# First block of a two-block network: attention passes begin after four of eight input projections, with the rest set between the passes

## The chip, the cores and the metric

One core of a Trainium2 chip runs the whole kernel in one launch. The metric is the time of one execution on the device in microseconds (us); the span is the time from the first to the last instruction of a profiled execution.

## The reference, cut to what matters

Two blocks work on 256 tokens of width 1024. The first (`first_block`) is computed once; its token mixing is what the change is about:

```python
mod = jax.nn.silu(c) @ w_ada[l] + b_ada[l]            # 6 rows of 1024: shifts, scales, gates
h  = rmsnorm(x,  g_mix[l]) * (1.0 + sc1) + sh1
hc = rmsnorm(xc, g_mix[l]) * (1.0 + csc1) + csh1      # 256 context tokens, used as keys and values
p = h @ w_in                                          # 1024 -> 2048
qa = axial_rope(heads(OFF_AQ, OFF_AK, A_HEADS, A_DH), rows, cols)   # 8 query heads of 64
ka = axial_rope(heads(OFF_AK, OFF_AV, A_KV, A_DH), rows, cols)      # 2 key heads of 64
ya = window_sink_attn(qa, ka, va, ka_c, va_c, sink)   # 128-token blocks, window 128, and 256 context keys
yb = chunk_gmlp(p[..., OFF_BU:OFF_BV], p[..., OFF_BV:OFF_CQ], ws, bs, gtok)
yc = diff_out(diff_attn(q1, q2, k1, k2, vall, lam), gsub, lam_init)  # 4 heads, two softmaxes each
y = jnp.concatenate([ya, yb, yc], axis=-1) @ w_out
x = x + gt1 * y
x = x + gt2 * hier_moe(h2, ...)                       # 16 experts, 2 of a group per token
```

The second block has two layers, each a SwiGLU FFN (1024 to 2 x 2816), a token mixing with three attentions (its q, k, v projection is 12 units of 256 columns) and another FFN. Each layer's nine modulation rows come from `cond @ ada_w[l] + ada_b[l]`. Everything is fp32.

## The kernel before, in words

Weights are streamed from memory by one DMA queue, issued by SyncE in an order that is written out. A *unit* is 128 x 2048 fp32 (1 MB). ScalarE rounds it (`conv_hi`, L270), VectorE makes the rest (`conv_lo`, L276), and TensorE multiplies in three products (`mm3`, L343 to L345). Three units fit (`RING`), so the load of unit c waits for `conv_lo` of unit c-3.

The modulation rows of both blocks (12 + 36 *halves* of 512 outputs) are made from a stream of its own. A half is 2 MB in two parts, and each part has one buffer, `ada[:, 0]` and `ada[:, 1]`, which it must leave before the next half can be loaded into it. For halves 0 to 3, TensorE multiplies directly (L1109). For all later ones VectorE does eight steps of 128x512 (`half_step`, L304 and L310), then TensorE sums over the partitions with four one-column products (`half_sum`, L324; each fp32 product stands as two rows in the trace), and VectorE adds the bias (`half_out`, L338). They are placed beside other work: halves 4 to 9 beside the early projections, 10 to 19 beside the attention passes, the rest beside the FFNs of the second block.

The input projection of the first block is eight units (`IN_UNITS`): 0 gives keys and values A, 1 and 2 the queries A, 3 keys C, 4 values C, 5 queries C, 6 and 7 the inputs of the gated MLP. Units 0, 3 and 4 are also multiplied with the context, so there are eleven projections of two tiles. Units 0 to 5 (`EARLY_UNITS`) come first. GpSimd rotates queries and keys (`rope`), TensorE turns them (`turn_pair`, L1137), and then 32 attention passes run, one per head and query block: 16 of kind A (the window) and 16 of kind C (the two softmaxes). Iteration i of the loop issues on TensorE the scores of pass i (L1158, in kind A behind a mask product L1157 of 512 columns), the turning of the probabilities of pass i-1 (L1165), and the product with the values of pass i-2 (L1174). VectorE takes the maximum (L1493), ScalarE the exponential (L1280) and the copy (L1287). In kind A query and key stand on 64 rows, since a head is 64 wide. Between the passes stand the projections of units 6 and 7 (`B_TURNS`), the turning of queries and keys C (from iteration `C_TURN0`), the gated MLP, the half sums (`ATT_SUMS`), and on VectorE some two or three half steps each. After the last pass of a group of eight, `finish` scales the output; behind the last one and behind the last half sum TensorE turns the result (`turn`, L409) and multiplies with `w_out`. TensorE executes its instructions in order; so do the others.

In the second block the loops over FFN groups and over q, k, v units are hardware loops (`Fori`).

## Time and profile before

| | us |
|---|---|
| median of 3 runs (lowest to highest) | 2260.92 (2258.34 to 2265.45) |
| the profiled execution | 2261.06 |
| its span | 2259.3 |
| busy: TensorE, VectorE, ScalarE, GpSimd | 2008.0, 1388.1, 998.5, 91.7 |
| mean granted TensorE clock | 0.924 of 2.4 GHz |

The span holds the whole program; the first block's mixing takes about its first 335 us. Shares of busy time are averages over stages with different limits, so each stage has to be read by itself. A TensorE that is busy at half clock counts as busy. The clock has two levels in the trace, written 1.00 and 0.50.

### The profile page before, as it was taken

To read this page: it belongs to the slowest core of one execution; us is meant where nothing else is said; L and a number is where in the kernel's file an instruction comes from. 1 tells how busy PE (TensorE), PEld (TensorE's weight loads), DVE (VectorE), ACT (ScalarE), POOL (GpSimd) and SP (SyncE) were. 2 spreads that over 40 slices of the span, in tenths; PEclk is the share of its full clock that TensorE was granted. 3 is DMA by queue.
4 is the path that set the end of the run, shared out by engine and by line. 5 is a ranking of instruction groups with operands and counts; after the bars stand their busy time and mean duration, and the time that the engine had idled before them with its cause. 6 is when DMAs were issued, how large, how long until landed. Compare 5 with 4: busy or idle time off the path is not lost.

```text
span 2259.3 us, 31283 instructions
## 1 busy us (share of the span) xinstructions
PE 2008.0 (89%) x12630; PEld 1769.3 (78%) x12630; DVE 1388.1 (61%) x1440; ACT 998.5 (44%) x1149; POOL 91.7 (4%) x103
## 2 busy tenths in 40 slices
PE   6878977999999699988797799989998979968997
PEld 1855667888888699978776689978997967857997
DVE  0875755899998677754433677766765343355445
ACT  2423324777777433344345343343334433444333
POOL 0230010000000100010000000000001000000000
PEclk9876786999999899989898899999999989989999
DMA  7563452899998287634312457755763532223553
GB/s 271 199 231 111 164 207 76 324 370 358 348 352 337 114 322 297 254 124 174 106 63 75 149 220 282 283 218 208 299 238 131 176 109 108 75 77 133 191 183 150
DMA packets 63845, 457.93 MB, mean 203 GB/s; under 512 B 7040, under 2 KB 7296, under 8 KB 8832
## 3 DMA queue, kind: packets, MB, share of 16 engines
q1 hardware_dynamic: 63744, 456.51, 53.4%
q8 instruction: 72, 1.18, 0.2%
q14 instruction: 29, 0.24, 0.0%
HBM read 455.43 MB, written 1.05 MB: 202 GB/s over the span
## 4 chain that ended last, share of the span: by engine, by line
issue 40%; PE 39%; DVE 10%; ACT 5%; DMA 3%; POOL 1%; DVEq 1%; POOLq 1%; SPq 0%; ACTq 0%
PE PS L343 10%; PE PS L344 10%; PE PS L345 10%; DVE wlo L276 3%; ACT whi L270 3%; DVE acc L310 2%; DMA ada<-in_ada 2%; PE PS L1158 1%; PE PS L324 1%; DMA raw<-in_stream 1%; PE PS L1701 1%; PE PS L1109 1%; PE PS L1174 1%; POOLq L396 1%; POOL st L397 1%
## 5 line engine op out<-in xcount | busy, mean ns | idle before, releaser
L276 DVE TENSOR_TENSOR wlo<-raw,whi 128x2048 fp32r<-128x2048 f32 x285 | 653.7, 2295 | 514.3 <-ACT whi L270 514.3
L270 ACT ACTIVATE whi<-raw 128x2048 fp32r<-128x2048 f32 x285 | 545.0, 1913 | 496.9 <-PE PS L345 461.1
L343 PE MATMUL PS<-whi,hhi 128*128 128x256 f32 (+1 forms) x1360 | 450.6, 331 | 18.1 <-DVE hlo L466 8.6
L344 PE MATMUL PS<-wlo,hhi 128*128 128x256 f32 (+1 forms) x1360 | 441.4, 325 | 0.0
L345 PE MATMUL PS<-whi,hlo 128*128 128x256 f32 (+1 forms) x1360 | 441.3, 324 | 0.0
L343 PE MATMUL PS<-hhi,whi 128*128 128x256 f32 x1408 | 402.2, 286 | 10.3 <-DVE mod L338 7.7
L344 PE MATMUL PS<-hlo,whi 128*128 128x256 f32 x1408 | 400.2, 284 | 0.0
L345 PE MATMUL PS<-hhi,wlo 128*128 128x256 f32 x1408 | 400.1, 284 | 0.0
L343 PEld LDWEIGHTS PS<-whi,hhi 128*128 128x128 f32 x1360 | 266.5, 196 | 41.1 <-DVE hlo L466 10.1
L343 PEld LDWEIGHTS PS<-hhi,whi 128*128 128x128 f32 x1408 | 272.0, 193 | 14.2 <-DVE wlo L276 8.9
L345 PEld LDWEIGHTS PS<-whi,hlo 128*128 128x128 f32 x1360 | 265.6, 195 | 19.2
L344 PEld LDWEIGHTS PS<-wlo,hhi 128*128 128x128 f32 x1360 | 266.5, 196 | 17.7
L344 PEld LDWEIGHTS PS<-hlo,whi 128*128 128x128 f32 x1408 | 272.1, 193 | 1.4
L345 PEld LDWEIGHTS PS<-hhi,wlo 128*128 128x128 f32 x1408 | 272.0, 193 | 0.0
L343 PE MATMUL PS<-whi,zr 128*128 128x512 f32 (+2 forms) x624 | 233.0, 376 | 21.0 <-DVE zr L1936 11.1
L310 DVE SCALAR_TENSOR_TENSOR acc<-ada,cs,acc 128x512 f32<-128x512 f32 x308 | 238.6, 775 | 10.8 <-DMA ada<-in_ada 1.4
L345 PE MATMUL PS<-whi,zr 128*128 128x512 f32 (+2 forms) x624 | 228.4, 369 | 0.0
L344 PE MATMUL PS<-wlo,zr 128*128 128x512 f32 (+2 forms) x624 | 228.2, 369 | 0.0
L343 PEld LDWEIGHTS PS<-whi,zr 128*128 128x128 f32 (+1 forms) x624 | 114.8, 184 | 41.7 <-DVE zr L1936 11.2
L345 PEld LDWEIGHTS PS<-whi,zr 128*128 128x128 f32 (+1 forms) x624 | 114.7, 184 | 20.8
L344 PEld LDWEIGHTS PS<-wlo,zr 128*128 128x128 f32 (+1 forms) x624 | 114.9, 184 | 18.8
L276 DVE TENSOR_TENSOR wlo<-ada,whi 128x2048 fp32r<-128x2048 f32 x48 | 109.9, 2292 | 12.7 <-ACT whi L270 12.5
(349 smaller groups left out, 1895.5 us busy)
## 6 DMA issues: line engine op xcount, KB each, us to landing
raw<-in_stream SPq DMA_DIRECT2D x285, 1024.0 KB, 4.8
ada<-in_ada SPq DMA_DIRECT2D x96, 1024.0 KB, 4.8
ada<-in_stream SPq DMA_DIRECT2D x48, 1024.0 KB, 4.9
xs<-in_x SPq DMA_DIRECT2D x1, 1024.0 KB, 7.7
Z<-in_ctx SPq DMA_DIRECT2D x1, 1024.0 KB, 9.8
masks<-in_masks SPq DMA_DIRECT2D x2, 512.0 KB, 6.8
Z<-in_gfinal SPq DMA_DIRECT2D x2, 512.0 KB, 7.4
y_out<-Z SPq DMA_DIRECT2D x2, 512.0 KB, 2.6
```

What stands on the lines that cost most here:

```text
L270: nc.scalar.activation(whi[:, s], src, ACT.Copy).then_inc(hi_ready, 1)
L276: nc.vector.tensor_tensor(wlo[:, s], src, whi[:, s].bitcast(F32), ALU.subtract).then_inc(lo_ready, 1)
L310: ins = nc.vector.scalar_tensor_tensor(a, w, c, a, ALU.mult, ALU.add)
L324: ins = nc.tensor.matmul(PS[:, bank, c:c + 1], acc[:, v % 2, c * P:(c + 1) * P], ones[:, 0:1], start=True, stop=True)
L343: nc.tensor.matmul(out_, ah, bh, start=start, stop=False, skip_group_check=check)
L344: nc.tensor.matmul(out_, ah, bl, start=False, stop=False, skip_group_check=check)
L345: return nc.tensor.matmul(out_, al, bh, start=False, stop=stop, skip_group_check=check)
L396: pool.drain()
L397: nc.gpsimd.tensor_tensor(st[:, 4 + t:5 + t], st[:, 2 + t:3 + t], k1[:, K1["half"]][:, 0:1], ALU.pow).then_inc(*N.rstd.up)
L1109: ins = nc.tensor.matmul(PS[0:2, 6 + v % 2, :], cs[:, n:16:8], ada[:, i, 512 * k:512 * k + 512], start=n == 0, stop=n == 7)
L1158: nc.tensor.matmul(PS[:, i % 2], q, k, start=i >= 16, stop=True).then_inc(*s_mm.up)
L1174: ins = nc.tensor.matmul(PS[:, 4 + (p // 8) % 2, 64 * (p % 8):64 * (p % 8) + 64], pt[:, p % 2, c * P:(c + 1) * P], v[c], start=c == 0, sto ...
```

## The change

1. Only units 0 to 3 are projected before the first pass. Units 4 to 7 (ten tiles) stand between the passes, in iterations 0 to 10 (`FILL_TURNS`), all through PSUM bank 7. SyncE's order of loads follows.
2. VectorE rotates the queries and keys A; GpSimd keeps those of C, in two pieces.
3. The keys of each kind-A head are held in a tile of their own, filled up to 128 rows with zeros, so that all scores have 128 rows. The mask product comes behind the scores and has 256 columns.
4. Halves 4 to 10 are done as before (three steps per iteration, up to half 10). Halves 11 to 17 (`SPLIT_HALVES`) are shared: VectorE does the first part (two steps per iteration, from iteration 16), TensorE the second with sixteen one-column products (`half_direct`, eight per iteration, from iteration 17), and four that add VectorE's part (`half_rest`). Halves 18 and 19 move: the first FFN of layer 0 takes 18 to 27, and 28 and 29 stand in layer 0's q, k, v projection.
5. The turning of C's queries and keys, the gelu and the gated MLP stand five or six iterations later.
6. The hardware loops of the second block are written out.

The diff, cut to its core:

```diff
-EARLY_HALVES = 20
-FFN_HALVES = {(0, 0): (20, 10), (0, 1): (30, 10), (1, 0): (40, 8), (1, 1): (48, 0)}
+EARLY_HALVES = 18
+SPLIT_HALVES = range(11, EARLY_HALVES)
+FFN_HALVES = {(0, 0): (18, 10), (0, 1): (30, 10), (1, 0): (40, 8), (1, 1): (48, 0)}
+QKV_HALVES = (28, 29)
...
+        ak = [z(6656, 512).rearrange("p (s n) -> p s n", s=2), xn[:, :, 768:1024]]
...
+        def half_free(v, i):
+            if v < PE_HALVES:
+                return ada_used_pe, 2 * v + i + 1
+            if v in SPLIT_HALVES and i:
+                return ada_used_pe, pe_used(v) + 1
+            return ada_used, dve_used(v) + i + 1
...
+        def half_direct(pe, v, bank, m):
+            cond = 0 if v < B1_HALVES else 16
+            if m == 0:
+                pe.wait_ge(ada_landed[1], 16 * (v + 1))
+                pe.wait_ge(*ada_out.at(v - PE_HALVES - 1))
+            c, k = m // 4, m % 4
+            ins = nc.tensor.matmul(PS[:, bank, c:c + 1], ada[:, 1, 512 * k + P * c:512 * k + P * c + P],
+                                   cs[:, cond + 4 + k:cond + 5 + k], start=m == 0, stop=False, skip_group_check=True)
+            if m == 15:
+                ins.then_inc(ada_used_pe, 1)
+        def half_rest(pe, v, bank):
+            pe.wait_ge(*half_free(v, 0))
+            for c in range(4):
+                ins = nc.tensor.matmul(PS[:, bank, c:c + 1], acc[:, v % 2, c * P:(c + 1) * P], ones[:, 0:1],
+                                       start=False, stop=True, skip_group_check=True)
+            ins.then_inc(*ada_sum.up)
...
-        EARLY_UNITS = 6
+        EARLY_UNITS = 4
...
-        B_TURNS = {0: (6, 0), 1: (6, 1), 3: (7, 0), 4: (7, 1)}
-        C_TURN0, GELU_TURN, GM_TURN = 6, 6, 12
+        ATT_V0, ATT_FULL = PE_HALVES + 1, SPLIT_HALVES[0]
+        ATT_STEPS = 3
+        SPLIT_PE, SPLIT_DVE = 17, 15
+        FILL_TURNS = {0: (4, "c", 0), 1: (4, "c", 1), 2: (4, "x", 0), 3: (4, "x", 1), 5: (5, "x", 0), 6: (5, "x", 1),
+                      7: (6, "x", 0), 8: (6, "x", 1), 9: (7, "x", 0), 10: (7, "x", 1)}
+        C_TURN0, GELU_TURN, GM_TURN = 11, 12, 18
...
-                    if i < 16:
-                        nc.tensor.matmul(PS[:, i % 2], idb[:, :], masks[:, i // 8], start=True, stop=False)
-                    nc.tensor.matmul(PS[:, i % 2], q, k, start=i >= 16, stop=True).then_inc(*s_mm.up)
+                    ins = nc.tensor.matmul(PS[:, i % 2], q, k, start=True, stop=i >= 16, skip_group_check=i < 16)
+                    if i < 16:
+                        ins = nc.tensor.matmul(PS[:, i % 2, 256:512], idb[:, :], masks[:, i // 8, 256:512], start=False, stop=True,
+                                               skip_group_check=True)
+                    ins.then_inc(*s_mm.up)
...
+                h, r = divmod(i - SPLIT_PE, 2)
+                if 0 <= h < len(SPLIT_HALVES):
+                    for m in range(8 * r, 8 * r + 8):
+                        half_direct(pe, SPLIT_HALVES[h], 6, m)
+                    if r:
+                        half_rest(pe, SPLIT_HALVES[h], 6)
...
+            for v, units in ((4, (3,)), (5, (4,)), (6, (5, 6, 7)), (7, (8, 9)), (8, (10,)), (9, (11,))):
+                for u in units:
+                    load(sp, u)
                 load_half(sp, v)
```

The three places where the order matters most follow.

TensorE at the start of the passes before. L343 to L345 are the last products of unit 5, L324 two half sums, L1137 the turning of queries and keys A, L1157 the mask, L1158 the first scores:

```order
L343 MATMUL PS<-whi,hhi 128x256
L344 MATMUL PS<-wlo,hhi 128x256
L345 MATMUL PS<-whi,hlo 128x256
L324 MATMUL PS<-k,acc 128x1 x8
L1137 MATMUL PS<-k,Z 128x128 x12
L1157 MATMUL PS<-masks,idb 128x512
L1158 MATMUL PS<-Z 128x512
```

The same place now. L372 to L374 are the last products of unit 3, and those with zr belong to unit 4 and the context:

```order
L373 MATMUL PS<-wlo,hhi 128x256
L374 MATMUL PS<-whi,hlo 128x256
L1146 MATMUL PS<-k,Z 128x128 x12
L338 MATMUL PS<-k,acc 128x1 x4
L1168 MATMUL PS<-Z 128x512
L1170 MATMUL PS<-masks,idb 128x256
L372 MATMUL PS<-whi,zr 128x256
```

The first scores now stand ahead of units 4 and 5, and the mask product behind them.

TensorE in the kind-C passes before (scores, turning, values, and every third or fourth pass a half sum):

```order
L1158 MATMUL PS<-Z 128x512
L1165 MATMUL PS<-k,Z 128x128 x4
L1174 MATMUL PS<-Z 128x64 x4
L324 MATMUL PS<-k,acc 128x1 x4
L1158 MATMUL PS<-Z 128x512
L1165 MATMUL PS<-k,Z 128x128 x4
L1174 MATMUL PS<-Z 128x64 x4
```

The same passes now, two of them, which make up one shared half:

```order
L1168 MATMUL PS<-Z 128x512
L1179 MATMUL PS<-k,Z 128x128 x4
L1188 MATMUL PS<-Z 128x64 x4
L349 MATMUL PS<-cs,ada 128x1 x8
L1168 MATMUL PS<-Z 128x512
L1179 MATMUL PS<-k,Z 128x128 x4
L1188 MATMUL PS<-Z 128x64 x4
L349 MATMUL PS<-cs,ada 128x1 x8
L358 MATMUL PS<-k,acc 128x1 x4
```

Twenty one-column products stand in two passes, where four stood in three or four.

VectorE beside the early projections before (L276 is `conv_lo`, L304 and L310 are the steps of a half):

```order
L276 TENSOR_TENSOR wlo<-raw,whi 128x2048
L304 TENSOR_SCALAR acc<-ada,cs 128x512
L310 SCALAR_TENSOR_TENSOR acc<-ada,cs,acc 128x512 x7
L276 TENSOR_TENSOR wlo<-raw,whi 128x2048
L304 TENSOR_SCALAR acc<-ada,cs 128x512
L310 SCALAR_TENSOR_TENSOR acc<-ada,cs,acc 128x512 x7
```

Now, from the `conv_lo` of unit 4 on; L748 to L754 are a rotation:

```order
L278 TENSOR_TENSOR wlo<-raw,whi 128x2048
L325 SCALAR_TENSOR_TENSOR acc<-ada,cs,acc 128x512 x4
L748 TENSOR_TENSOR Z<-Z,k 128x128
L749 TENSOR_TENSOR Z<-Z,k 128x128
```

One half instead of six is done there, and three rotations stand between the conversions.

## Rows read from the trace of the kernel before

**Rows 1.** Stages: us, busy by engine (instructions), granted clock, DMA share, GB/s.
```profile
143.90:183.60 39.70, 34.42 (x202) 25.07 (x202) 19.99 (x35) 12.48 (x24) 0.00 (x0) 0.93 0.34 122
183.60:240.80 57.20, 53.03 (x174) 35.61 (x175) 29.40 (x63) 19.45 (x44) 1.66 (x1) 0.50 0.30 106
240.80:291.40 50.60, 46.38 (x277) 35.32 (x277) 40.52 (x71) 20.96 (x50) 1.02 (x1) 0.89 0.52 187
...
1000.00:1035.00 35.00, 35.00 (x294) 35.00 (x293) 14.20 (x7) 14.38 (x12) 0.00 (x0) 1.00 0.50 184
```

**Rows 2.** Timeline of ScalarE, early projections: start, us, instruction, idle before and releaser.
```profile
91.11 0.60 ACT L1252 ACTIVATE Z<-PS 128x512 f32<-128x512 f32 x1 [3.36 <-PE PS L345]
97.59 1.92 ACT L270 ACTIVATE whi<-raw 128x2048 fp32r<-128x2048 f32 x1 [5.88 <-DMA raw<-in_stream]
```

**Rows 3.** Timeline of VectorE, early projections and passes.
```profile
115.73 5.54 DVE L310 SCALAR_TENSOR_TENSOR acc<-ada,cs,acc 128x512 f32<-128x512 f32 x7
...
178.13 2.29 DVE L276 TENSOR_TENSOR wlo<-raw,whi 128x2048 fp32r<-128x2048 f32 x1 [3.62 <-ACT whi L270]
...
218.03 0.69 DVE L1493 TENSOR_REDUCE sm<-PS 128x1 f32<-128x512 f32 x1 [3.33 <-PE PS L1158]
```

**Rows 4.** Timeline of TensorE, start of the passes.
```profile
136.78 1.84 PE L324 MATMUL PS<-k,acc 128*128 128x1 f32 x8 [9.75 <-DVE mod L338]
...
143.87 0.58 PE L1157 MATMUL PS<-masks,idb 128*128 128x512 bf16 x1 [2.59 <-issue]
```

**Rows 5.** Timeline of TensorE, kind-A passes at the low clock.
```profile
224.51 2.07 PE L1158 MATMUL PS<-Z 64*128 64x512 f32 x2
...
229.02 0.63 PE L1157 MATMUL PS<-masks,idb 128*128 128x512 bf16 x1
...
234.09 0.63 PE L1157 MATMUL PS<-masks,idb 128*128 128x512 bf16 x1
```

**Rows 6.** Timeline of TensorE, kind-C passes at the high clock.
```profile
245.02 1.08 PE L1158 MATMUL PS<-Z 128*128 128x512 f32 x2
245.94 0.60 PE L1165 MATMUL PS<-k,Z 128*128 128x128 f32 x4
...
247.21 1.08 PE L1158 MATMUL PS<-Z 128*128 128x512 f32 x2
...
251.64 1.00 PE L324 MATMUL PS<-k,acc 128*128 128x1 f32 x8
252.50 1.10 PE L1158 MATMUL PS<-Z 128*128 128x512 f32 x2
```

**Rows 7.** The chain of waits, a load of one part of a half.
```profile
253.19 4.75 DMA ada<-in_ada
```

**Rows 8.** Timeline of TensorE, last scores and the end of the passes.
```profile
286.50 1.08 PE L1158 MATMUL PS<-Z 128*128 128x512 f32 x2
...
302.58 1.86 PE L324 MATMUL PS<-k,acc 128*128 128x1 f32 x8 [10.09 <-DVE acc L310]
304.31 3.65 PE L409 MATMUL PS<-k,xn 128*128 128x128 f32 x16
```

**Rows 9.** Timeline of TensorE, around two falls of the clock.
```profile
277.53 1.12 PE L1165 MATMUL PS<-k,Z 128*128 128x128 f32 x4 [3.56 <-ACT Z L1280]
...
389.33 2.29 PE L877 MATMUL PS<-sm,Z 128*128 128x4 f32 x20
```

**Rows 10.** Stretches around a rise and a fall, and narrow products; columns as in rows 1.
```profile
283.00:284.00 1.00, 1.00 (x12) 1.00 (x10) 0.96 (x2) 1.00 (x3) 0.00 (x0) 1.00 0.01 0
...
355.00:361.00 6.00, 6.00 (x29) 6.00 (x29) 0.00 (x0) 0.00 (x0) 0.00 (x0) 0.50 0.35 145
388.00:389.00 1.00, 1.00 (x6) 0.84 (x5) 0.40 (x1) 1.00 (x1) 0.00 (x0) 1.00 1.00 426
392.00:393.00 1.00, 1.00 (x7) 1.00 (x6) 1.00 (x2) 0.00 (x0) 0.00 (x0) 0.50 0.39 148
```

More of the change, by code:

```diff
@@ L632, in hidden_act @@
             act_hi(act, 0, None, E0, h0)
[L633 removed]
+            for g in range(1, FFN_GROUPS):
+                steps, sums = g < nh, g <= nh
+                c = at_gate(c0, g)
+                conv_hi(act, c + RING, E0)
+                act_silu(act, g, c0, E0, h0)
+                conv_hi(act, c + 1 + RING, E0)
+                act_hi(act, g, c - 1, E0, h0)
+                conv_hi(act, c + 2 + RING, E0)
         def hidden_dve(dve, c0, E0, h0, halves):
             v0, nh = halves
[L638 to L650 removed]
             conv_lo(dve, c0 + RING, E0)
@@ L659, in hidden_dve @@
                 half_steps(dve, v0, 1)
-            hidden_loop(dve, body, nh)
+            for g in range(1, FFN_GROUPS):
+                steps, sums = g < nh, g <= nh
+                c = at_gate(c0, g)
+                conv_lo(dve, c + RING, E0)
+                if steps:
+                    half_steps(dve, v0 + g, 0)
+                dve_h(dve, g, h0)
+                conv_lo(dve, c + 1 + RING, E0)
+                dve_lo(dve, g, h0)
+                if sums:
+                    half_out(dve, v0 + g - 1, 2 * (1 - g % 2))
+                if steps:
+                    half_steps(dve, v0 + g, 1)
+                conv_lo(dve, c + 2 + RING, E0)
         N1, N3 = Norm("n1", 3), Norm("n3", 2, stats_only=True)
@@ L745, in a_scores @@
             if p < 16:
-                r = slice(64 * (j % 2), 64 * (j % 2) + 64)
                 kv = j % 2
@@ L1258, in turned_out @@
                 act.wait_ge(*t1_mm.at(i))
+                if i < 2:
+                    for kv in range(2):
+                        r = slice(64 * kv, 64 * kv + 64)
+                        ins = nc.scalar.activation(ak[kv][r, i], PS[r, bank, 0:256], ACT.Copy)
+                    ins.then_inc(*t1_out.up)
+                    return
                 if i not in (8, 11):
@@ L1415, in normalise_v @@
                 dve.drain()
-                sq = xn[:, :, 0:256]
+                sq = row[:, 0:512].rearrange("p (t n) -> p t n", t=2)
+                dve.wait_ge(*rope_c.at(1))
                 for t in range(NT):
@@ L1617, in pe_layer @@
                 project(unit(pe, QK0 + j, E0), hhi, hlo, j, lo_at=None if j else lo_at(1, l)).then_inc(unit_used, 1)
-            with pe.Fori(0, 3) as i:
-                for j in range(3):
-                    pe.wait_ge(B["q_out"].sem, l * 12 + i * 3 + (j + 1))
-                    project(unit(pe, QK0 + 3 + j, E0 + i), hhi, hlo, j).then_inc(unit_used, 1)
+            for j in range(3, 12):
+                pe.wait_ge(*B["q_out"].at(j - 3, l))
+                project(unit(pe, QK0 + j, E0), hhi, hlo, j % 3).then_inc(unit_used, 1)
+                if l == 0 and j in (6, 10):
+                    half_sum(pe, QKV_HALVES[j // 10], 3)
             def gate_unit(f, bank, tile=None):
@@ L1886, in dve_layer @@
             conv_lo(dve, FF0 + FFN_UNITS - 1 + RING, E0)
-            with dve.Fori(0, 4) as i:
-                for j in range(3):
-                    conv_lo(dve, QK0 + j + RING, E0 + i)
+            for j in range(12):
+                conv_lo(dve, QK0 + j + RING, E0)
+                if l == 0 and 1 <= j <= 8:
+                    v, n = QKV_HALVES[(j - 1) // 4], 2 * ((j - 1) % 4)
+                    if n == 6 and v > QKV_HALVES[0]:
+                        half_out(dve, v - 1, 3)
+                    half_step(dve, v, n)
+                    half_step(dve, v, n + 1)
+            if l == 0:
+                half_out(dve, QKV_HALVES[1], 3)
             dve.wait_ge(*B["q_out"].at(11, l))
@@ L2121, in _ @@
                 hidden_sp(sp, FF0, E0, FFN_HALVES[l, 0])
-                with sp.Fori(0, MIX_UNITS // RING) as e:
-                    for j in range(RING):
-                        load(sp, QK0 + RING + j, E0 + e)
+                for j in range(MIX_UNITS):
+                    if l == 0 and j in (1, 5):
+                        load_half(sp, QKV_HALVES[j // 5])
+                    load(sp, QK0 + RING + j, E0)
                 hidden_sp(sp, FF1, E0, FFN_HALVES[l, 1])
```

336 lines of the change are left out of this document (159 added, 177 removed).

## The prediction

> **What bounds the kernel now.** I read the stages first (the stretches with busy time and clock), then the timelines of single engines in the first 310 us, and the chain of waits for what a DMA costs there. Nearly all of the change lies in that part.
>
> In the passes TensorE is busy 34.42 of 39.70 us, then 53.03 of 57.20, then 46.38 of 50.60, and its clock is 0.93, 0.50 and 0.89 [rows 1]. So the middle stretch is TensorE at half clock: one kind-A pass takes 5.07 us (229.02 to 234.09), its scores on 64 rows 2.07 [rows 5]. A kind-C pass at the high clock takes 2.19 us, 245.02 to 247.21, and there VectorE works 40.52 of 50.60 us [rows 1, 6]. Ahead of the passes TensorE waits for VectorE: 9.75 us before a half sum, first mask at 143.87 [rows 4]. Behind them it waits 10.09 us for the last half, and turns the result at 304.31 [rows 8]. These two waits and the low clock can be won back. The reader should keep four marks: first pass 143.87, scores of pass 17 at 245.02, of pass 31 at 286.50, turning at 304.31.
>
> **The change part by part.** I build the same four marks for the changed kernel.
>
> *The start.* The fourth of the six projections that remain is copied out at 91.11 [rows 2]; one takes about 5.8 us (rows 2: idle 3.36 and what ScalarE does between), so unit 3 with its context ends at 91 + 2 x 5.8 = 102.6. Then the last rotation on VectorE decides. It stands behind the `conv_lo` of unit 5, whose load is queued on SyncE behind the second part of half 5, and that waits for four steps of half 4, which stand behind a rotation of about 3 us (twelve instructions, my estimate from the 0.69 us of 512 columns in rows 3: 0.25 each). Before, this unit landed at 97.59 [rows 2]; five later, say 103. With the two conversions (1.92 and 2.29, rows 2 and 3) and 3.2 us of rotation it is 110; turning, a half sum at the low clock (1.73: 302.58 to 304.31, rows 8) and the copies add 2.5. First pass at 112.7; bounds 108 (load in time) and 117.
>
> *Passes 0 to 10.* A warm pass is 2.19 plus about 0.2 for the shorter mask, a tile of 24 products 2.88 (half of 5.8). Eleven passes and ten tiles: 11 x 2.4 + 28.8 = 55. On top come 3.5 for the cold start; three waits of 1.6 us where bank 7 must be copied out before the next unit's first tile (4.8); and the units' conversions: VectorE waited 3.62 us for `conv_hi` and worked 2.29 [rows 3], three such places with three steps of 0.79 (5.54 / 7, rows 3) behind them, of which tiles hide part; 2 us are left. Pass 11 starts at 112.7 + 65 = 178; bounds 172 and 184.
>
> *Passes 11 to 16* are a chain of latencies, not of work: the turning of C's queries waits for the copy, that for exponential and copy of the same pass. Before the chain took 5.7 us a pass at low clock; warm I get 4.4, since scores, turning and values halve. Two dearer passes: iteration 11 waits for the copy of unit 7's last tile (6.2), iteration 12 sits behind a `conv_hi` and the gelu with its table loads (12). The four others 5.2 each. Together 39, scores of pass 17 at 217; bounds 209 and 224. Before: 245.02 [rows 6]. This is the gain, 28 us, and it comes from the earlier start (31 us) less 17 us of projections, plus the clock: with 128 rows in the scores I expect it to come back sooner than in rows 5.
>
> *Passes 17 to 30, the shared halves.* Four one-column products cost 0.86 us at the high clock (251.64 to 252.50, rows 6) and 1.73 at the low one [rows 8]. A shared half stands in two passes with 16 + 4 products, that is five times as much: warm 2 x 2.19 + 5 x 0.86 = 8.7 us, low 2 x 4.5 (5.07 less 0.6 of mask, rows 5) + 5 x 1.73 = 17.6. Seven halves: 61 or 123 us. Before, these fourteen passes took 286.50 - 245.02 = 41.5 us. So even at its best TensorE loses 19.5 us here, since it was nearly full already [rows 1] and VectorE's relief (four steps of 0.79 a half) buys nothing.
>
> Two things come on top. First, the second part of a half now leaves its buffer only with TensorE's sixteenth product, and the next half's is wanted one pass later, after 0.86 + 2.19 = 3.05 us. A load takes 4.75 us from issue to landing [rows 7]: a wait of 1.7 us in six of seven halves, 10 us; warm 10.4 a half, 71 in all. At the low clock the pass hides it. Second, the clock. It fell at about 392, after 2.15 us of four-column products and the narrow turnings behind them, with TensorE never idle (1.00 at 388, 0.50 at 392; rows 9, 10); it stayed at 0.50 for the six us of twenty-column products at 355, busy 6.00 of 6.00 [rows 10]. After the fall before 277.53 it was back by 283 with plain kind-C passes [rows 9, 10]. The new stretch mixes the two: 2.6 us of one-column products and 1.7 us of waiting, then a wide score product. I expect it to fall in nearly every half and to rise again in many, and take 13.3 us a half, between 10.4 and 17.6, a little on the warm side because of the quick return at 283: 7 x 13.3 = 93 us.
>
> The Trainium skill, "TensorE: Matmul & The Clock Gate", Part 1, says the gate follows how busy the engine has been and that what throttles it is idleness. Read so, one-column products without gaps would keep the clock high, and the sum would be the one with 71 us. The rows at 355 and 392 speak against reading busy that way, so it is a rival and not the forecast.
>
> *The end.* No step is left over behind the last pass. Before, scores of pass 31 to turning were 17.8 us [rows 8]. Now: 0.9, then 4.2 for the rest of the pipeline, 5.3 for `finish`: 10.4.
>
> *The moved halves.* Two in the first FFN change nothing in its count of ten. The two in q, k, v add 16 steps to a VectorE that is busy 14.20 of 35 us, and eight products to a TensorE that is busy 35.00 of 35.00 [rows 1]: 2 x 0.86 = 1.7 us. Writing out the loops: there is no idle time in that stretch, itself a loop, so nothing; bounds minus 2 and plus 2. GpSimd's rotations end long before C's turning; their bound is one pass, 5 us, inside those of pass 17.
>
> **Sum.** Turning at 217 + 93 + 10.4 = 320.4 against 304.3: plus 16.1, with q, k, v plus 17.8. On the profiled execution's own 2261.06 us: 2279. It is 0.1 us above the median of the runs shown, so nothing is corrected. In general the result is 2261 + (X - 75), where X is the time of passes 17 to 30; equality needs X = 75, 10.7 us a half.
>
> **The rivals.**
> - *The clock holds, the loads are late.* X = 71.4, minus 4: 2257. For it: the clock stood at 0.93 in the first stretch with half sums and 64-row scores. Against: those had tiles of 24 products between them [rows 1]. By the page named above this is what would come; by the rows I give it 0.2.
> - *The clock holds and the loads are in time* (shorter latency with an empty queue, or TensorE late enough elsewhere). X = 61, minus 14, 2247; with pass 17 at 212 it is 2242. For it: nothing else uses the queue there. Against: 4.75 us was measured in the same stretch with little else moving. 0.2.
> - *The clock stays low through all shared halves.* X = 123, plus 48: 2309. It decides if kind-C scores can't lift the clock with narrow products between them. For it: 57.20 us at 0.50 in rows 1 with TensorE 93% busy. Against: the return by 283. 0.15.
> - *The start is not earlier*, because the rotation on VectorE and the loads of units 5 to 7 push the first pass towards 125: plus 12 on any of the above. Inside the range, no chance of its own.
>
> **How the numbers follow.** Forecast 0.45, rivals 0.2, 0.2 and 0.15. This kernel can't be told from no change within 0.3%, 6.8 us. Faster by more (below 2254): nearly all of the second rival, a quarter of the first, and a slice of the forecast where pass 17 comes at 209 and a half costs 11: 0.27. Slower: most of the forecast and all of the third, 0.57. Within: 0.16. The range reaches from 2245 to 2308: both ends are the rivals', and the likeliest case alone would be 2262 to 2292.
>
> **What would show it.** Right: first scores near 113; pass 17 near 217; between there and pass 31 a clock that changes often, mean 0.6 to 0.85, and 90 us; waits of TensorE for DMA at the first product of each shared half where the clock is high; no wait ahead of the turning. Wrong: a clock of 1.00 throughout passes 17 to 30 (then X is 61 or 71), or one of 0.50 from pass 12 to the end (then it is over 2300), or kind-A passes with 128 rows that still run at the low clock, which would move pass 17 to 224.

## The result, and the profile after

The changed kernel takes 2302.38 us (median of 4 runs, 2297.17 to 2309.96) against 2259.63 for the kernel before (2256.13 to 2265.45): ratio 1.0182, 95% interval 1.0149 to 1.0216, slower. The forecast of 2279 had the sign and its range held the time, but the loss is 43 us where 18 were forecast. The profiled execution took 2306.45 us, with a span of 2304.7 and a mean granted clock of 0.909.

The four marks of the prediction come first, on TensorE's timeline of the changed kernel (start, us, instruction, idle before and who ended it). They are the first scores, the scores of pass 17, the scores of pass 31 and the turning; in the kernel before they stand at 143.87 and 286.50 to 304.31 [rows 4, 8], pass 17 at 245.02 [rows 6].

```profile
110.51 1.12 PE L1146 MATMUL PS<-k,Z 128*128 128x128 f32 x4 [8.93 <-DVE Z L754]
112.98 2.05 PE L1168 MATMUL PS<-Z 128*128 128x512 f32 x2
...
217.68 1.91 PE L1168 MATMUL PS<-Z 128*128 128x512 f32 x2
...
335.10 2.06 PE L1168 MATMUL PS<-Z 128*128 128x512 f32 x2
...
348.93 3.46 PE L438 MATMUL PS<-k,xn 128*128 128x128 f32 x15 [5.16 <-DVE xn L1535]
```

The first pass starts 31 us earlier than before and pass 17 still 27 us earlier. Then passes 17 to 30 take 335.10 - 217.68 = 117.4 us, where they took 41.5 before [rows 6, 8]. The turning comes 348.93 - 304.31 = 44.6 us late, and that is nearly the whole of the 45.4 us by which the two profiled executions differ. The stages, in the columns of rows 1:

```profile
113.00:184.20 71.20, 62.38 (x426) 54.05 (x426) 41.33 (x70) 23.28 (x47) 10.01 (x17) 0.93 0.45 171
184.20:217.70 33.50, 23.70 (x103) 17.75 (x104) 22.65 (x42) 14.23 (x28) 1.66 (x1) 0.65 0.40 139
217.70:232.00 14.30, 13.96 (x82) 11.64 (x81) 5.16 (x10) 3.91 (x10) 0.00 (x0) 0.74 0.21 75
232.00:335.10 103.10, 103.10 (x413) 89.42 (x413) 27.25 (x53) 15.19 (x36) 1.02 (x1) 0.50 0.37 133
335.10:354.80 19.70, 14.54 (x63) 13.21 (x64) 7.12 (x16) 4.25 (x8) 2.90 (x2) 0.50 0.00 1
```

From 232 on TensorE is busy for 103.10 of 103.10 us, and all of it at the lower of its two levels. It waits for nothing and doesn't come back to 1.00. In the first shared half, before 232, the clock still went both ways: it is 1.00 from 222 to 225, 0.50 from 226 to 228 and 1.00 again from 229 to 232, with the same one-column groups standing there. VectorE, which was relieved, works 27 of these 103 us. One shared half in that stretch, on TensorE's timeline of the changed kernel:

```profile
232.70 2.05 PE L1168 MATMUL PS<-Z 128*128 128x512 f32 x2
234.55 1.06 PE L1179 MATMUL PS<-k,Z 128*128 128x128 f32 x4
235.40 1.81 PE L1188 MATMUL PS<-Z 128*128 128x64 f32 x8
237.00 3.52 PE L349 MATMUL PS<-cs,ada 128*128 128x1 f32 x16
240.38 2.05 PE L1168 MATMUL PS<-Z 128*128 128x512 f32 x2
242.23 1.06 PE L1179 MATMUL PS<-k,Z 128*128 128x128 f32 x4
243.08 1.81 PE L1188 MATMUL PS<-Z 128*128 128x64 f32 x8
244.68 3.52 PE L349 MATMUL PS<-cs,ada 128*128 128x1 f32 x16
248.06 1.84 PE L358 MATMUL PS<-k,acc 128*128 128x1 f32 x8
249.77 2.06 PE L1168 MATMUL PS<-Z 128*128 128x512 f32 x2
```

A half takes 249.77 - 232.70 = 17.07 us. Its one-column products (L349 and L358) hold 8.9 us of it, and the two passes the rest, each piece at about double the time of the high clock [rows 6].

### The profile page after: what moved, and what is told of

The parts are those of the page before. It is cut to its first block, busy times and chain, and to the rows that moved or that the text cites. A ratio compares the mean times of both kernels' runs of the same rounds, so it can differ in the third digit from the quotient of the medians.

```text
span 2304.7 us, 30222 instructions
## 1 busy us (share of the span) xinstructions
PE 2065.4 (90%) x12854; PEld 1832.5 (80%) x12854; DVE 1366.9 (59%) x1448; ACT 998.6 (43%) x1151; POOL 76.1 (3%) x105
## 4 chain that ended last, share of the span: by engine, by line
PE 43%; issue 39%; DVE 8%; ACT 5%; DMA 2%; POOL 1%; DVEq 1%; POOLq 1%; SPq 0%; ACTq 0%
PE PS L372 10%; PE PS L374 10%; PE PS L373 10%; DVE wlo L278 3%; ACT whi L272 3%; PE PS L349 2%; PE PS L1168 2%; PE PS L1188 1%; DMA ada<-in_ada 1%; PE PS L1761 1%; DMA raw<-in_stream 1%; DVE acc L325 1%; PE PS L1123 1%; PE PS L338 1%; PE PS L1179 1%
## 5 line engine op out<-in xcount | busy, mean ns | idle before, releaser
L372 PE MATMUL PS<-whi,hhi 128*128 128x256 f32 (+1 forms) x1360 | 451.5, 332 | 22.4 <-DVE hlo L495 8.9
L374 PE MATMUL PS<-whi,hlo 128*128 128x256 f32 (+1 forms) x1360 | 441.6, 325 | 0.0
L372 PE MATMUL PS<-hhi,whi 128*128 128x256 f32 x1408 | 402.2, 286 | 8.0 <-DVE mod L367 5.9
L374 PE MATMUL PS<-hhi,wlo 128*128 128x256 f32 x1408 | 400.4, 284 | 0.0
L372 PEld LDWEIGHTS PS<-whi,hhi 128*128 128x128 f32 x1360 | 266.2, 196 | 45.5 <-DVE hlo L495 10.5
L372 PEld LDWEIGHTS PS<-hhi,whi 128*128 128x128 f32 x1408 | 272.2, 193 | 11.9 <-DVE mod L367 7.2
L374 PEld LDWEIGHTS PS<-whi,hlo 128*128 128x128 f32 x1360 | 265.5, 195 | 19.4
L373 PEld LDWEIGHTS PS<-wlo,hhi 128*128 128x128 f32 x1360 | 266.3, 196 | 17.8
L374 PEld LDWEIGHTS PS<-hhi,wlo 128*128 128x128 f32 x1408 | 272.2, 193 | 0.0
L372 PE MATMUL PS<-whi,zr 128*128 128x512 f32 (+2 forms) x624 | 233.8, 377 | 21.0 <-DVE zr L2004 11.1
L374 PE MATMUL PS<-whi,zr 128*128 128x512 f32 (+2 forms) x624 | 229.1, 370 | 0.0
L325 DVE SCALAR_TENSOR_TENSOR acc<-ada,cs,acc 128x512 f32<-128x512 f32 x280 | 210.5, 752 | 9.3 <-DMA ada<-in_ada 1.3
L372 PEld LDWEIGHTS PS<-whi,zr 128*128 128x128 f32 (+1 forms) x624 | 115.2, 185 | 42.4 <-DVE zr L2004 11.2
L374 PEld LDWEIGHTS PS<-whi,zr 128*128 128x128 f32 (+1 forms) x624 | 114.8, 184 | 20.8
```

The costliest lines, as they stand in the source:

```text
L325: ins = nc.vector.scalar_tensor_tensor(a, w, c, a, ALU.mult, ALU.add)
L372: nc.tensor.matmul(out_, ah, bh, start=start, stop=False, skip_group_check=check)
L373: nc.tensor.matmul(out_, ah, bl, start=False, stop=False, skip_group_check=check)
L374: return nc.tensor.matmul(out_, al, bh, start=False, stop=stop, skip_group_check=check)
```

## The experiments

The theory: one-column products fill TensorE's time and carry almost no streaming, so the clock falls, doesn't return, and every pass pays double; and, a separate effect, the filled keys keep the clock up in the kind-A passes. The main rival: it is only the products' own time. In each diff below the `+` lines are the edit. In the table X is the time from the scores of pass 17 to those of pass 31, and the clock is the granted one in that stretch; both come from the one profiled execution, which can lie some us off the median (for the kernel with 3 wide products it was the slowest, 2299.04 us, and so it was for the last row, 2251.00). A clock between 0.50 and 1.00 is the mean of stretches at either level. The ratio is to the kernel before, in the same batch of runs; between batches that kernel's own median moved from 2259.63 to 2263.67, so small differences are read from the ratios. Pass 17 stands at 217.5 to 221.5 in kernels whose TensorE does the same up to there (after, both with wide products, the other shape), so a difference of 4 us at this mark says nothing.

| kernel | median us | ratio, interval | pass 17 at | X | clock in X |
|---|---|---|---|---|---|
| before | 2259.63 | | 245.0 | 41.5 | 0.92 |
| after | 2302.38 | 1.0182 (1.0149 to 1.0216) | 217.7 | 117.4 | 0.53 |
| after, 3 wide products per group | 2289.82 | 1.0104 (1.0078 to 1.013) | 221.5 | 111.6 | 0.72 |
| after, 1 wide product per group | 2283.76 | 1.0102 (1.0073 to 1.0131) | 217.5 | 94.7 | 0.75 |
| after, halves not shared | 2250.13 | 0.9945 (0.9929 to 0.9962) | 217.9 | 51.9 | 0.90 |
| the same, keys of 64 rows | 2256.19 | 0.9968 (0.9957 to 0.9979) | 224.3 | 51.5 | 0.87 |
| before, keys filled, mask cut | 2251.05 | 0.9953 (0.9936 to 0.9969) | 228.2 | 42.0 | 0.96 |
| before, keys filled, mask whole | 2251.28 | 0.9943 (0.9926 to 0.996) | 232.9 | 43.2 | 0.92 |
| before, keys filled, one-column products added | 2294.40 | 1.0142 (1.011 to 1.0174) | 230.2 | 84.1 | 0.70 |
| before, keys filled, wide products added | 2250.58 | 0.9938 (0.9919 to 0.9956) | 229.5 | 47.7 | 1.00 |
| after, shared halves in another shape | 2264.77 | 1.001 (0.9997 to 1.0024) | 220.8 | 83.3 | 0.92 |
| not shared, steps uneven | 2242.94 | 0.991 (0.9888 to 0.9932) | 224.3 | 51.8 | 0.84 |
| the same, 20 wide ahead of the turning | 2238.83 | 0.9897 (0.9872 to 0.9921) | 223.5 | 51.6 | 0.84 |
| the same, and 2 wide behind each pass from 21 on | 2241.50 | 0.9902 (0.9881 to 0.9922) | 223.0 | 59.7 | 0.84 |

**Work added to the changed kernel.** Three wide bf16 products, never read, behind every 4 direct products (m counts them in a half):

```diff
+                    def wide():
+                        if i >= 21:
+                            for _ in range(3):
+                                nc.tensor.matmul(PS[:, 7], idb[:, :], masks[:, 1], start=True, stop=True)
                     for m in range(8 * r, 8 * r + 8):
                         half_direct(pe, SPLIT_HALVES[h], 6, m)
+                        if m % 4 == 3:
+                            wide()
                     if r:
                         half_rest(pe, SPLIT_HALVES[h], 6)
+                        wide()
```

> The changed kernel with work ADDED: from iteration 21 of the attention loop on, after every 4 direct products of the modulation and after each half's rest, 3 products of 128 rows and 512 columns (bf16, into bank 7, never read). My theory (the clock): after 232 us every pass runs at granted clock 0.50 because the one-column and 20-column products hold TensorE's time without streaming anything, so the clock never comes back although TensorE waits for nothing. Wide columns between them should bring it back: 335.10 - 217.68 = 117.4 us should fall by 15 to 30 us although about 50 x 3 x 0.22 us = 20 to 30 us of products are added, total 2275 to 2290 against 2302 of the changed kernel. Rival (the sum of TensorE's work, not the clock: the direct products cost what their weight loads cost at any clock): the added products only lengthen it, by 20 us at high clock to 60 us at low, 2320 to 2360. Second rival (the low clock in these passes has another cause, such as a limit on power): clock stays 0.50, plus 40 to 60 us.

And the same with `range(1)`:

> As the run with three wide products at each place, but one at each: the dose. The clock theory: this is too little to turn the clock in most halves, so it stays at 0.50 for much of the stretch and the total is 2295 to 2320 (the changed kernel 2302), clearly above the run with three. The rival (work alone): a third of the cost of the run with three, 2308 to 2322, and less than that run.

Both kernels do more work than the changed one and are faster, by 13 and 19 us in the medians and by 0.8% each in the ratios. That rules out the rival that only the sum of work counts, and the one that the low clock has a cause outside these products. Their stretches X, with three products and with one:

```profile
221.50:333.10 111.60, 107.41 (x562) 84.97 (x568) 32.34 (x63) 19.08 (x46) 1.02 (x1) 0.72 0.37 133
217.50:312.20 94.70, 90.14 (x512) 77.27 (x518) 32.56 (x63) 19.10 (x46) 1.02 (x1) 0.75 0.42 157
```

I was wrong on the dose: one product lifts the clock from 0.53 to 0.75, as much as three (0.72). Which of the two is the better kernel isn't shown, since their intervals are nearly the same. Neither brings the clock to 1.00: with three products TensorE still spent 238 to 265 us wholly at the low level before the clock rose, and then it went back and forth. Here is one group with a single wide product, from the timeline of that kernel on TensorE:

```profile
259.07 1.05 PE L349 MATMUL PS<-cs,ada 128*128 128x1 f32 x8 [1.32 <-DMA ada<-in_ada]
259.98 0.38 PE L1221 MATMUL PS<-masks,idb 128*128 128x512 bf16 x1
260.20 0.95 PE L349 MATMUL PS<-cs,ada 128*128 128x1 f32 x8
```

At the high clock the 16 rows take 2.0 us where they took 3.52, and a wait for the load appears, which the low clock had hidden.

**The cause put into a kernel that hasn't the change.** Into the kernel before with filled keys, 8 one-column products per pass, or 4 wide ones:

```diff
+                if i >= 17:
+                    if i == 17:
+                        pe.wait_ge(*yb_done.at(0))
+                    for _ in range(8):
+                        nc.tensor.matmul(PS[:, 7, 0:1], ident, ones[:, 0:1], start=True, stop=True)
```

```diff
+                    for _ in range(4):
+                        nc.tensor.matmul(PS[:, 7], idb[:, :], masks[:, 1], start=True, stop=True)
```

> The kernel before with filled keys (the run 'padding alone', 2251 us, passes 17 to 31 in 42.0 us, granted clock 0.96) with work ADDED: 8 products of a 128x128 f32 tile by one column after each pass from 17 to 31 and the two iterations behind them, never read: the shape of the changed kernel's direct products, nothing else of the change. One such group of 8 takes about 0.97 us at high clock (1.81 for 15 in the changed kernel), 17 of them 16 us. My theory (a product of one column holds TensorE and streams nothing, so the clock falls and then every pass is longer): passes 17 to 31 take 65 to 85 us and the total rises by 25 to 45 us. Rival (only the work itself costs, the clock is held by the passes): 42 + 14 = 56 us at most, granted clock over 0.90, total plus 10 to 17.

> As the run with 8 one-column products per pass, but the same time on TensorE at high clock filled with streaming: 4 bf16 products of 128x512 into bank 7 (about 0.22 us each, 0.9 us per pass). Clock theory: the granted clock stays at 0.95 or more, passes 17 to 31 take 54 to 57 us, total plus 12 to 15 us against padding alone, clearly less than the one-column run. Rival (any added TensorE time does the same): equal to the one-column run within 5 us.

The one-column kernel's timeline on TensorE shows the fall:

```profile
240.49 1.00 PE L324 MATMUL PS<-k,acc 128*128 128x1 f32 x8
241.35 1.93 PE L1208 MATMUL PS<-k 128*128 128x1 f32 x16
243.14 1.10 PE L1155 MATMUL PS<-Z 128*128 128x512 f32 x2
244.08 0.89 PE L1166 MATMUL PS<-k,Z 128*128 128x128 f32 x4
244.76 1.80 PE L1175 MATMUL PS<-Z 128*128 128x64 f32 x8
246.36 3.52 PE L1208 MATMUL PS<-k 128*128 128x1 f32 x16
249.74 2.05 PE L1155 MATMUL PS<-Z 128*128 128x512 f32 x2
```

After 2.8 us of one-column products without a gap the clock falls inside the next pass. It doesn't stay down for good here: with a group in every pass it is back at 1.00 from 270 to 278, and then at 0.50 from 280 to 304. The windows of the two kernels over X, first one-column, then wide:

```profile
230.20:314.30 84.10, 84.10 (x455) 72.48 (x454) 37.14 (x65) 19.09 (x46) 1.02 (x1) 0.70 0.32 113
```

```profile
229.50:277.20 47.70, 45.86 (x286) 32.62 (x285) 36.52 (x64) 19.02 (x46) 1.02 (x1) 1.00 0.54 185
```

My expectation had one group at half its price (8 products are 16 rows and take 1.93 us, not 0.97). So of the 84.1 - 42.0 = 42.1 us in X, 14 x 1.9 = 27 are the products at the high clock, and the other 15 are the low clock; as 4.6 us of X were idle on TensorE without the products and none are with them, the low clock's part may be up to 20. The total rose by 43 us, within what I expected. The wide products, 4 to a pass, took 1.03 us a group, lengthened X by 5.7 us and cost the kernel nothing (2250.58 against 2251.05, intervals overlap), where I had expected 12 to 15 us. The two additions are therefore not the same time on TensorE, 1.93 against 1.03 us a pass. What they show is the direction: from 0.96 the one kind takes the clock down to 0.70 and the other up to 1.00.

**The sharing undone.** VectorE makes all eight steps of halves 11 to 17, and everything else of the change stays:

```diff
-SPLIT_HALVES = range(11, EARLY_HALVES)
+SPLIT_HALVES = range(EARLY_HALVES, EARLY_HALVES)
...
-        ATT_V0, ATT_FULL = PE_HALVES + 1, SPLIT_HALVES[0]
+        ATT_V0, ATT_FULL = PE_HALVES + 1, EARLY_HALVES
```

> The changed kernel with one part undone: halves 11 to 17 are no longer shared; VectorE does all 8 steps of each (3 per iteration, 104 over 35 iterations), TensorE only the 4 sums of each. Everything else (first pass at 113 us, filled keys, units between the passes) stays. Theory (the direct products with their low clock are the whole loss): passes 17 to 31 take 45 to 70 us in place of 117.4, a step of VectorE at 0.64 us is 1.9 us per iteration beside 3.8 us a pass or less, so VectorE may set a pass of 4 to 4.5 us; turning begins at 285 to 300, total 2240 to 2262, level with or ahead of the kernel before (2260). Rival (the loss lies in the early start itself: VectorE is behind in its modulation steps and everything that waits for it shifts): turning begins no earlier than 330, total 2285 or more.

As the theory had it: 52 us come off the changed kernel, and it is 12 us ahead of the kernel before. Its stage X:

```profile
217.90:269.80 51.90, 42.58 (x246) 31.86 (x245) 41.51 (x76) 18.18 (x44) 1.02 (x1) 0.90 0.56 200
```

VectorE has 41.51 us of work in X, where the kernel before has 34.2, and X is 10 us longer than there.

**The same work in another shape.** To tell the products' own time from the clock, the 16 products of a shared half are turned round:

```diff
-            ins = nc.tensor.matmul(PS[:, bank, c:c + 1], ada[:, 1, 512 * k + P * c:512 * k + P * c + P],
-                                   cs[:, cond + 4 + k:cond + 5 + k], start=m == 0, stop=False, skip_group_check=True)
+            if m % 4:
+                return
+            k = m // 4
+            ins = nc.tensor.matmul(PS[0:1, bank, 8:512], cs[:, cond + 4 + k:cond + 5 + k], ada[:, 1, 512 * k + 8:512 * k + 512],
+                                   start=k == 0, stop=k == 3)
```

> The changed kernel with the 16 one-column products of a shared half put the other way round: 4 products with the modulation's input as the one-column side that is loaded and 504 columns of the projection's weights streaming past it. About the same time on TensorE at high clock (a f32 product of 512 columns takes 1.0 to 1.1 us as two records of the scores show, so 4.0 to 4.3 us a half against 2 x 1.9 us). The result of these 4 products is a row that is NOT turned into columns and added: TensorE's share of halves 11 to 17 is left out of the modulation. Theory (shape: what fills TensorE's time without streaming lets the clock fall): if one loaded column is enough for streaming to count, passes 17 to 31 take 65 to 80 us in place of 117.4, total 2250 to 2270. Rival 1 (the columns streamed past a one-column weight count as little as one column streamed past 128): clock 0.53 as before and 4 products at low clock of 2.05 us each, 2 x 4.4 + 8.2 + 1.8 = 18.8 us a half, 130 us, total 2310 to 2320. Rival 2 (the number of products alone decides): between these.

The first theory holds in its clock and total. Two products (four rows) take 1.85 us at the high clock, and eight of one column 1.84 to 1.93, so TensorE's time for them is the same; the clock in X is 0.92 in place of 0.53, and the kernel is 37.6 us faster (2264.77 against 2302.38). Two of its groups, and X:

```profile
250.30 2.48 PE L351 MATMUL PS<-ada,cs 128*1 128x504 f32 x4 [1.74 <-DMA ada<-in_ada]
256.07 1.85 PE L351 MATMUL PS<-ada,cs 128*1 128x504 f32 x4
...
220.80:304.10 83.30, 72.58 (x326) 37.66 (x324) 32.52 (x63) 19.08 (x46) 1.02 (x1) 0.92 0.49 178
```

The edit changes more than what streams: there are 4 products in place of 16, and TensorE loads one column for each of them in place of 128 (its loads are busy for 37.66 us in X, and for 101.06 in the changed kernel). The runs don't tell these apart. X was 83.3, a little over what I gave, because of waits for DMA. They are the ones that the prediction put at 1.7 us in six of seven halves. TensorE's waits of this kernel from 220 to 304 us (in total, times, longest):

```profile
PE PS L351 <- DMA ada<-in_ada: 10.4, 6, 1.8
```

The rest, 2264.77 - 2250.13 = 14.6 us, is what the sharing costs with the clock restored, those waits among it, less what turning the row would cost, which is left out here.

**Filled keys alone, and undone.** Into the kernel before:

```diff
-                return aq[r, j // 2, t * P:(t + 1) * P], ak[r, :], v
+                return aq[:, j // 2, t * P:(t + 1) * P], ak[kv], v
...
+            nc.gpsimd.memset(ak[0][64:128], 0.0)
+            nc.gpsimd.memset(ak[1][0:64], 0.0).then_inc(*const_made.up)
```

> The kernel BEFORE with one part of the change alone: keys filled with zeros up to 128 rows and the mask product cut to its last 256 columns and put behind the scores; no direct products, no reordering, modulation wholly on VectorE. If filling the rows is what keeps the clock up (64 rows count for less than 128), the low stretch 183 to 245 us of the kernel before shortens and the kernel becomes 10 to 25 us faster (2235 to 2250). If rows don't matter: the masks save 16 x 0.11 us, at the low clock twice that, and GpSimd's two fills cost nothing on the path: 2256 to 2262, no change. If the two fills of 64 x 512 or 64 rows that GpSimd gets ahead of its rope are on the path to the first pass, it is up to 5 us slower.

The same with the mask of 512 columns ahead of the scores again:

> Padding alone (2251) with the mask put back as in the kernel before: 128x512 ahead of the scores. Against padding alone it shows what the narrower mask gives, against the kernel before what the filled keys give by themselves. Theory (the filled rows keep the clock): nearly all of the 12.6 us come from the rows: 2250 to 2255, and the wide mask may even help the clock. Rival (the narrower, later mask gave it, since the scores no longer wait behind it): 2257 to 2263.

Both are 11 to 13 us faster than the kernel before. The reader should look at the granted clock in passes 8 to 16 of three kernels: before, filled keys with the whole mask, filled keys with the mask cut.

```profile
190.40:245.00 54.60, 53.52 (x174) 35.72 (x174) 27.95 (x59) 15.14 (x40) 1.66 (x1) 0.50 0.27 97
```

```profile
189.80:232.90 43.10, 35.88 (x175) 27.66 (x173) 26.47 (x58) 13.97 (x37) 1.66 (x1) 0.75 0.28 98
```

```profile
188.90:228.20 39.30, 31.13 (x175) 23.53 (x175) 26.12 (x58) 13.80 (x36) 1.66 (x1) 0.84 0.30 108
```

With the whole mask TensorE has the same products as before, and only zeros were added to them. The clock rises from 0.50 to 0.75, so about half of the low stretch of rows 1 is left. The narrower mask brings 4 us in this stretch of the profiled executions but none in the medians.

From the other side, the unshared kernel with keys of 64 rows again:

```diff
-                return aq[:, j // 2, t * P:(t + 1) * P], ak[kv], v
+                r = slice(64 * kv, 64 * kv + 64)
+                return aq[r, j // 2, t * P:(t + 1) * P], ak[r, :], v
```

> The unshared variant with a second part undone: keys of 64 rows as in the kernel before (the mask product stays 256 columns behind the scores, the first pass stays early). It shows what the early start gives alone, without filled keys. If filled rows keep the clock up: low clock comes back over passes 3 to 16, each pass with a projection or turning between takes 5.5 to 6.5 us, pass 17 comes at 225 to 240 in place of 217.9, total 2258 to 2275. If the rows don't matter because between these passes stand projections that stream enough: within 4 us of the unshared variant, 2246 to 2254.

The kernel loses 6 us (the intervals of the two ratios just touch), the clock of passes 0 to 16 goes from 0.87 to 0.79, and pass 17 comes at 224.3: between my two cases. Where projections stand between the passes, up to about 173, the clock is 0.89 against 0.91 with filled keys; behind that it is 0.67 against 0.81. So, in these two executions, the rows matter most where nothing wider stands between the passes.

**A version that beats both.** In the unshared kernel VectorE is still at its steps when the passes end, and idle for a third of the time before pass 17. The steps are laid out as 4 per iteration for the first 16, then 3:

```diff
-        ATT_SUMS = {(8 * k + 7) // ATT_STEPS + 2: ATT_V0 + k for k in range(ATT_FULL - ATT_V0)}
+        ATT_AT = [4 * min(i, 16) + 3 * max(i - 16, 0) for i in range(PASSES + 4)]
+        ATT_SUMS = {max(i for i in range(PASSES) if ATT_AT[i] <= 8 * k + 7) + 1: ATT_V0 + k for k in range(ATT_FULL - ATT_V0)}
```

> The unshared variant (2250 us; passes 17 to 31 in 51.9 us) with VectorE's modulation steps laid out unevenly: 4 per iteration in the first 16 (where VectorE idled 35 us of 103 us), 3 from there to iteration 28, so the last half is summed at iteration 30 rather than behind the loop. In the trace of the unshared variant TensorE waits 10.05 us for acc before the turning and VectorE's 6 steps and a 2.42 us wait for a transfer stand ahead of the last finish. Theory: VectorE sets the passes 17 to 31 and the wait; with 12 steps fewer behind pass 16, 12 x 0.64 = 8 us come off between pass 17 and turning, 2 to 4 of them given back in the early passes or to transfers: total 2242 to 2247. Rival: the transfers of the halves (8 queue waits) set the pace, then the early steps only wait for DMA and the passes before 17 get longer: 2248 to 2256.

The total came. From pass 17 to the turning it is 62.1 us in place of 71.9, about what I expected, but none of it is in X, which stays at 51.8: what went is the last half behind the passes, with its wait of 10.05 us. Pass 17 is 6.4 us later (224.3), so the profiled executions differ by 3.4 us only, and the medians by 7; the intervals of the two ratios touch, so that this kernel beats the unshared one is likely, and that it beats the kernel before is shown. The wait ahead of the turning is now 5.16 us, on `finish` alone:

```profile
286.42 3.68 PE L438 MATMUL PS<-k,xn 128*128 128x128 f32 x16 [5.16 <-DVE xn L1539]
289.88 2.83 PE L511 MATMUL PS<-Z,k 128*128 128x128 f32 x16
293.83 0.50 PE L372 MATMUL PS<-whi,hhi 128*128 128x512 f32 x1 [1.11 <-ACT row L516]
```

Into that wait go 20 wide products:

```diff
+            pe.wait_ge(*yb_done.at(0))
+            wide(20)
             pe.wait_ge(*o_out.at(3))
```

> The variant with uneven steps (2243; TensorE idle 5.16 us ahead of the turning of the attention's output, then low clock 284.9 to 291.7) with 20 useless bf16 products of 128x512 ADDED in that idle time (20 x 0.22 = 4.4 us at high clock). Theory: the clock stays high through turning and gate products, which take 3.68 and 2.83 us at the low clock: they save 2 to 3 us, total minus 1 to minus 3. Rival: the products reach over the end of the wait and add up to 2 us, or the saved time is only waiting for VectorE's hlo: no change within 1 us.

```profile
280.09 4.48 PE L1116 MATMUL PS<-masks,idb 128*128 128x512 bf16 x20
285.42 1.97 PE L438 MATMUL PS<-k,xn 128*128 128x128 f32 x16 [0.84 <-DVE xn L1545]
287.73 2.05 PE L511 MATMUL PS<-Z,k 128*128 128x128 f32 x16 [0.35 <-POOL Z L505]
290.90 0.50 PE L372 MATMUL PS<-whi,hhi 128*128 128x512 f32 x1 [1.11 <-ACT row L516]
```

Turning and gate products run at the high clock (1.97 and 2.05 us). From the start of the turning to the first product behind them (L372) it is 5.48 us in place of 7.41. That is 1.9 us, as expected; the median is 4 us less, at 2238.83, but the intervals of these two kernels overlap (0.9872 to 0.9921 and 0.9888 to 0.9932), so a gain in the total isn't shown. Two wide products per pass on top:

> As the run with 20 filler products ahead of the turning, and 2 more behind each pass from iteration 21 on (13 x 2 x 0.22 = 5.7 us of TensorE time added at high clock). In the variant with uneven steps 13.7 us of the passes 17 to 31 run at low clock and VectorE is busy for most of them, so TensorE's added time is partly hidden. Theory: the low clock in them goes, minus 2 to minus 5 us against that run. Rival: at 2 products it is only work, plus 1 to 4 us, since TensorE is the bound in the passes.

This measured 2241.50 (ratio 0.9902, 0.9881 to 0.9922): no difference from either. Its theory failed: the clock in X stayed at 0.84 and X grew from 51.6 to 59.7 us. So two wide products behind each pass, in a kernel without the one-column groups, did not bring the clock back; useless products are a test, and not a sure remedy. The best kernel is 0.9897 of the kernel before, 1% faster.

## Why the prediction was right and wrong, step by step

- *The start.* Right in the path and, by luck, in the number: first pass forecast 112.7, measured 112.98. The last rotation (L754) is what TensorE waits for. But unit 5 was converted from 100.29 on and not from 103, and its twelve rotating instructions took 6.0 us (104.44 to 110.46) in place of the 3.2 that I put at 0.25 each. Those of the rotation before took 0.28 each with GpSimd idle; these took 0.53, while GpSimd rotated the keys C (103.25 to 110.3). The two errors cancel. ScalarE's conversion and one instruction of each rotation on VectorE:

```profile
100.29 1.91 ACT L272 ACTIVATE whi<-raw 128x2048 fp32r<-128x2048 f32 x1 [10.47 <-DMA raw<-in_stream]
...
93.24 0.28 DVE L750 TENSOR_TENSOR Z<-Z,k 128x128 f32<-128x128 f32 x1
...
105.37 0.53 DVE L750 TENSOR_TENSOR Z<-Z,k 128x128 f32<-128x128 f32 x1
```
- *Passes 0 to 16.* Right: pass 11 forecast 178, measured 179.96; pass 17 forecast 217, measured 217.68. The waits for bank 7 were put at 1.6 us each and measured 1.52, 1.53 and 1.53; the wait at iteration 12 is 5.99 us. Passes 11 to 16 took 37.7 us against 39, although their clock was 0.65 and not the high one that the sum assumed.
- *Passes 17 to 30.* This step failed: "I expect it to fall in nearly every half and to rise again in many, and take 13.3 us a half". Only the first half went so, with a clock of 0.74. The clock fell for good at 232, and a half took 17.07 us. X was 117.4 against 93, which is 24.4 of the 27.6 us that were missing in span (45.4 against 17.8). The all-low bound worked out for this case, 17.6 a half and the third rival's 2309, was right within 3 us of the profiled execution. The rows for that rival were on the table ([rows 10]: 0.50 over six us of twenty-column products, TensorE always busy), and I gave it 0.15 since the clock came back at 283 with plain kind-C passes. But between 277.53 and 283 no one-column product stood on TensorE at all, and that fall came in 3.56 us of idleness. A return seen without the disturbing work says little on a return with it. The runs with added products show that the kind of product does this: 8 one-column products a pass lower the clock to 0.70, 4 wide ones raise it to 1.00.
- *The warm price of sharing.* Right in kind: forecast 61 us of TensorE work for seven halves, plus 10 us of waits for the second part of a half. The waits stood nowhere in the changed kernel, since the low clock hid them, but with the clock back they are 10.4 us in 6 places. Sharing would have lost even at the high clock: the other shape still loses 14.6 us to the unshared kernel.
- *The end.* Forecast 10.4, measured 348.93 - 335.10 = 13.8. The missing 3.4 us are the low clock again: values and turning at double time (3.51 for 16 rows of L1188, 1.99 in the kernel with uneven steps).
- *Filled keys.* Under-used: the prediction said only that the clock would "come back sooner". Alone they are worth 12 us, as much as the unshared kernel gains in all. The gains don't add up: the unshared kernel with keys of 64 rows still gains 0.3%, about 7 us. The early start of the passes, 28 us, shows at pass 17 as 10 us (217.9 against 228.2) and is given back in X (51.9 against 42.0), where VectorE then does the halves that it did ahead of the passes before. Scores of pass 31 stand at 269.8 with it and at 270.2 without.
- *The moved halves.* Right: q, k, v of layer 0 takes 65.18 us in place of 63.35, plus 1.8 (forecast 1.7). The stretch with TensorE busy throughout:

```profile
1034.90:1100.10 65.20, 65.20 (x547) 65.20 (x546) 35.89 (x28) 26.51 (x22) 2.93 (x5) 1.00 0.57 211
```

No run has the loops written out alone, but nothing in the rest of the program points at them: the distance to the kernel before is 44.6 us at the turning, 43.6 at the start of q, k, v and 45.4 at its end and at the end of the program.

The Trainium skill, "TensorE: Matmul & The Clock Gate", Part 1, has the clock follow how busy the engine is, with idleness as what throttles it. For idleness the traces agree: a wait of 5.16 us leaves the turning at the low clock (3.68 us for its 16 rows), and filled with products it doesn't (1.97). For work they don't: the changed kernel's TensorE, busy for 103.10 of 103.10 us, stayed at 0.50, and with three wide products per group it was idle for 4.2 of 111.6 us and had the higher clock, 0.72. The measurement decides.

What stays open: why one wide product per group does as well as three, and why neither reaches 1.00; why the clock stayed down for 103 us in the changed kernel, when it came back several times in the kernel with one-column products added, which hold nearly the same share of a pass at the low clock (3.52 of 7.7 us against 8.9 of 17.07); and whether it is the single streamed column or the load of 128 columns ahead of it that counts for so little. It also wasn't tried to share the halves in the other shape with the row turned back, since the unshared kernel needs neither.

## What to carry to other kernels

Read a busy TensorE together with its granted clock, and price narrow products (one column, four columns, half-filled rows) twice: for their own time, and for the clock that they take from the work around them. Where a term of a sum has a low-clock and a high-clock price, don't take the middle; ask which of the two states can sustain itself with that mix of instructions, and add or remove a few useless wide products to find out. When a forecast mark is met, still check its terms, since two of them can be wrong and cancel. And work moved onto an engine that is nearly full, to relieve one that is not the bound, loses before the clock is even counted.

## What the runs showed of the hardware

- TensorE busy for 103.10 of 103.10 us stayed at the granted clock 0.50, with one-column products holding about half of its time (8.9 of 17.07 us a half).
- Useless work can make a kernel faster: one and three added products of 512 columns per group took 19 and 13 us off the changed kernel. It need not: two per pass in the best kernel left the clock at 0.84.
- Zeros in the unused 64 rows of a product lifted the granted clock of the same passes from 0.50 to 0.75.
- 504 columns streamed past one loaded column keep the clock (0.92), while one column past 128 loaded ones loses it (0.53), at the same time on the engine (1.85 us for two of the one, 1.84 to 1.93 for eight of the other).
- A rotating instruction on VectorE (two 128x128 fp32 operands) took 0.28 us with GpSimd idle and 0.53 while GpSimd ran the same kind of instruction at 0.46 to 0.50 us each.
